# Linear attention inside a fused eleven-stage network: decays, heads and the norm of the memory set in another order

## What is computed

```python
def first_block(x, mem, mem_norm_g, norm_mix_g, ab_w_in, gla_w_alpha2, ...):
    mem_n = rms_norm(mem, mem_norm_g)
    ...
            proj = xn @ ab_w_in[j]
            y_a = gla_group(proj[..., :GLA_COLS], gla_w_alpha2[j], gla_b_alpha[j], gla_norm_g[j])
    ...
        h = h + mixed @ w_mix_out[layer]
        h = h + memory_cross_attention(rms_norm(h, norm_xattn_g[layer]), mem_n,
                                       xattn_wq[layer], xattn_wkv[layer], xattn_wo[layer])
```

## Time and profile before

| | |
|---|---|
| median of three runs | 3285.48 us (3285.32 to 3285.83) |
| the profiled execution's own time | 3284.78 us |
| its span in the trace | 3283.0 us |
| mean granted clock of TensorE | 0.98 of full |
| busy: PE / PEld / DVE / ACT / POOL | 95% / 76% / 47% / 36% / 4% |
| bytes moved | 270.60 MB, 82 GB/s over the span |

### The profile page before, as it was taken

How to read it: one execution, slowest core, us unless ns; L and a number is a source line. 1 busy time by engine, 2 the same in 40 slices (tenths; PEclk the granted TensorE clock), 3 DMA queues, 4 the chain that set the end, 5 groups by cost and what they waited for, 6 DMA issues and landing times.

```text
span 3283.0 us, 39941 instructions
## 1 busy us (share of the span) xinstructions
PE 3114.7 (95%) x17208; PEld 2490.4 (76%) x17208; DVE 1558.8 (47%) x1957; ACT 1175.8 (36%) x1564; POOL 126.5 (4%) x142
## 2 busy tenths in 40 slices
PE   8889988799999989899999998899999999999999
PEld 6787766577887766777887785588888887878887
DVE  4444446546544664546544654543335343363333
ACT  4343332434322464344322544532224322342221
POOL 1010000100000100100000200000001000000000
PEclk9899999899999999999999999999999999999999
DMA  4333001213332321313332231033323212133321
GB/s 150 119 131 104 15 21 40 77 52 90 103 90 85 94 64 52 103 42 97 92 97 78 91 90 52 26 94 98 93 87 116 81 64 93 65 103 90 103 90 64
DMA packets 355617, 270.60 MB, mean 82 GB/s; under 512 B 28672, under 2 KB 341504, under 8 KB 355184
## 3 DMA queue, kind: packets, MB, share of 16 engines
q1 hardware_dynamic: 351504, 252.83, 25.8%
q0 software_dynamic: 3936, 15.22, 1.3%
HBM read 261.73 MB, written 6.29 MB: 82 GB/s over the span
## 4 chain that ended last, share of the span: by engine, by line
PE 84%; DVE 8%; ACT 5%; issue 1%; POOL 0%; DMA 0%; DVEq 0%; SPq 0%; ACTq 0%; POOLq 0%
PE ps L189 83%; ACT arena L203 2%; DVE arena L220 2%; ACT whi L206 1%; DVE arena L212 1%; DVE wlo L212 1%; PE ps L192 1%; DVE hT L212 1%; DVE sml L229 1%; DVE xlo L220 1%; DVE arena L216 1%; ACT arena L206 0%; DVE split L212 0%; ACT L203 0%; POOL arena L212 0%
## 5 line engine op out<-in xcount | busy, mean ns | idle before, releaser
L189 PE MATMUL ps<-xhi,whi 128*128 128x512 f32 (+2 forms) x2192 | 874.1, 399 | 12.3 <-DVE wlo L212 4.2
L189 PE MATMUL ps<-xhi,wlo 128*128 128x512 f32 (+2 forms) x2192 | 857.1, 391 | 0.0
L189 PE MATMUL ps<-xlo,whi 128*128 128x512 f32 (+2 forms) x2192 | 856.7, 391 | 0.0
L189 PE MATMUL ps<-split,whi 128*128 128x512 f32 (+2 forms) x2640 | 830.9, 392 | 14.7 <-DVE split L212 10.4
L212 DVE TENSOR_TENSOR wlo<-wraw,whi 128x2048 fp32r<-128x2048 f32 (+4 forms) x258 | 550.7, 2137 | 475.6 <-ACT whi L206 475.4
L189 PEld LDWEIGHTS ps<-split,whi 128*128 128x128 f32 (+1 forms) x2640 | 491.5, 189 | 143.1 <-issue 26.6
L206 ACT ACTIVATE whi<-wraw 128x2048 fp32r<-128x2048 f32 (+4 forms) x258 | 456.2, 1771 | 352.8 <-PE ps L189 342.9
L189 PE MATMUL ps<-split,wlo 128*128 128x512 f32 (+2 forms) x1320 | 509.8, 386 | 0.0
L189 PEld LDWEIGHTS ps<-xhi,whi 128*128 128x128 f32 (+2 forms) x2192 | 410.9, 187 | 119.1 <-issue 10.4
L189 PEld LDWEIGHTS ps<-xhi,wlo 128*128 128x128 f32 (+2 forms) x2192 | 410.5, 187 | 91.9 <-issue 5.9
L189 PEld LDWEIGHTS ps<-xlo,whi 128*128 128x128 f32 (+2 forms) x2192 | 410.3, 187 | 90.6
(11 more groups left out here) (110 smaller groups left out, 2041.3 us busy)
## 6 DMA issues: line engine op xcount, KB each, us to landing
wraw<-in_ffn_w_up SPq DMA_DIRECT2D x128, 512.0 KB, 5.2
wraw<-in_ffn_w_down SPq DMA_DIRECT2D x32, 1024.0 KB, 5.0
wraw<-in_odd_w_in SPq DMA_DIRECT2D x24, 1024.0 KB, 5.2
wraw<-in_ffn_w_gate SPq DMA_DIRECT2D x44, 512.0 KB, 3.9
wraw<-in_xattn_wkv SPq DMA_DIRECT2D x16, 1024.0 KB, 5.6
wraw<-in_xattn_wq SPq DMA_DIRECT2D x8, 1024.0 KB, 5.1
wraw<-in_xattn_wo SPq DMA_DIRECT2D x8, 1024.0 KB, 5.2
wraw<-in_cd_w_in SPq DMA_DIRECT2D x8, 1024.0 KB, 5.6
```

The costliest lines, as they stand in the source:

```text
L189: return self.e.matmul(out, lhsT, rhs, start=start, stop=stop, skip_group_check=True)
```

## The change

In the stage gla, and nowhere else:

- The memory is normed before it is turned, while its tokens lie on the partitions: ACT takes the squares of two 128x1024 tiles with a sum along the row, and the root of the 128x2 sums; DVE scales both tiles by it. PE turns them when both are scaled. ACT rounds each turned tile with the gain as its scale, DVE makes its rest. The squares, products with ones, and eight products of the class Norm are gone.
- The values' product has 512 columns: two units of 512x512 rows and columns, 96 products, added up in four banks over both units. Both pairs' la products stand in it behind the first token tile of the first unit. The DVE and ACT work of both pairs' decays (decay) is issued at this place, between the roundings and rests of the units.
- The turnings ke and the updates U of both pairs stand between the gates' blocks; states(0) before the memory's first block on DVE, states(1) behind it.
- The heads' parts s, o and sum are set behind the memory's blocks 0 to 9 by a list (heads), so that part o of a head is two or more blocks behind its s, and its sum two behind its o; the other 22 blocks follow without a break. s no longer waits for the states.
- ke, SS, pts, EL, the squares, the roots and the outputs have two buffers each, in part on tiles that are free by then (la, keT, t1, ep).

The diff cut to its core:

```diff
-            la, t1, t2, ep, keT, U, SS, pts = (al(T), al(T), al(T), al(T), al(512), al(1024), al(1024), al(512))
-            os_, EL = la, sml[:, 16:24]
+            la, t1, ep, *ke = (al(T) for _ in range(5))
+            keT, U, SS, pts = al(512), al(1024), [al(1024), al(1024)], [al(512), al(512)]
+            sqs, rss, oss = [t1, ke[1]], [ep, ke[0]], [la, keT]
-            u_v = tm_units("v", Wi, 512, 512, 4)
+            u_v = [(("v", "unit", n), [(Wi[n * 512:n * 512 + 512, 512:1024], 0)], 512) for n in range(2)]
+                return ((("s", 0),), (("s", 1),), (("o", 0),), (("s", 2), ("o", 1)), (("sum", 0),), (("s", 3), ("o", 2)),
+                        (("sum", 1),), (("o", 3),), (("sum", 2),), (("sum", 3),))
...
+                    pe.wait_ge(S.V.of("mem", 1), ps.empty("turn", k))
...
+                bs = [ps.take("v", i, of=(0, 1, 2, 3)) for i in range(4)]
+                for n, (name, parts, bn) in enumerate(u_v):
+                    u = W.take(name, parts, bn)
+                    for i in range(4):
+                        c = slice(i * P, (i + 1) * P)
+                        pe.wait_ge(W.ready(name), ps.empty("v", i))
+                        for k in range(4):
...
+                        elif i == 0:
+                            decay(0)
+                            decay(1)
...
+                gates = fm_tensor(pe, S, u_g, X8, norm.made, of=(4, 5, 6, 7))
+                for p in range(2):
+                    next(gates)
+                    turn(p)
+                    next(gates)
+                    updates(p)
+                blocks = memory.tensor(pe)
+                for parts in heads():
+                    next(blocks)
+                    for what, hd in parts:
+                        part(what, hd)
+                run(blocks)
...
+                for i in range(2):
+                    dve.wait_ge(S.A.of("mem_root"))
+                    dve.ts(mt[:, i, :], mt[:, i, :], mem_rs[:, i:i + 1], None, ALU.mult).then_inc(*up(S.V, "mem", i))
+                W.rest(dve, u_qk[1][0])
+                W.rest(dve, u_a[0][0])
+                for k in range(8):
+                    dve.wait_ge(S.A.of("mem_hi", k))
+                    dve.stt(mem[k].lo, ps.ap("turn", k)[:, 0:256], par_col("mem_norm_g", None, k), mem[k].hi.bitcast(F32),
+                            ALU.mult, ALU.subtract).then_inc(*up(S.V, "mem_lo", k, frees=("turn", k)))
+                W.rest(dve, u_v[0][0])
...
+                decay(0)
+                W.rest(dve, u_v[1][0])
+                decay(1)
+                W.rest(dve, u_g[0][0])
+                states(0)
+                W.rest(dve, u_g[1][0])
+                blocks = memory.vector(dve)
+                next(blocks)
+                states(1)
+                for n, parts in enumerate(heads()):
+                    if n:
+                        next(blocks)
+                    for what, hd in parts:
+                        part(what, hd)
...
+                act.wait_ge(l_mem.of("x"))
+                for i in range(2):
+                    act.act(SS[i], mt[:, i, :], ACT.Square, acc=mem_rs[:, i:i + 1]).then_inc(*up(S.A))
+                act.wait_ge(S.A.own())
+                rstd_scalar(act, S, mem_rs, P, 2, 1024, 1e-6, mem_rs, None).then_inc(*up(S.A, "mem_root"))
...
+                for k in range(8):
+                    act.wait_ge(S.P.of("turn", k))
+                    act.copy(mem[k].hi, ps.ap("turn", k)[:, 0:256], scale=par_col("mem_norm_g", None, k)).then_inc(
+                        *up(S.A, "mem_hi", k))
+                W.round(act, u_v[0][0])
...
+                decay(0)
+                W.round(act, u_v[1][0])
+                decay(1)
+                for i in range(4):
+                    act.wait_ge(S.P.of("v", i))
+                    act.copy(vT[:, i * T:(i + 1) * T], ps.ap("v", i)).then_inc(*up(S.A, "v", i, frees=("v", i)))
...
+                for p in range(2):
+                    W.round(act, u_g[p][0])
+                    gate(2 * p)
+                    act.wait_ge(S.P.of("ke", p), S.P.of("U", 0, 1) if p else NEVER)
                     act.copy(keT, ps.ap("ke", p)).then_inc(*up(S.A, "keT", p, frees=("ke", p)))
+                    gate(2 * p + 1)
...
+                    elif what == "sum":
+                        act.wait_ge(S.P.of("sum", hd), S.V.of("mix", hd - 2) if hd > 1 else NEVER)
+                        rstd_scalar(act, S, ps.ap("sum", hd), P, T, P, 1e-6, rss[hd % 2], None).then_inc(
                             *up(S.A, "root", hd, frees=("sum", hd)))
                         act.wait_ge(S.V.of("mix", hd))
+                        act.copy(mixA[hd].hi, oss[hd % 2]).then_inc(*up(S.A, "mix_hi", hd))
```

More of the change, by code:

```diff
@@ L1208, in tensor @@
             def tensor(pe):
[L1209 to L1227, removed]
+                def run(stream):
+                    for _ in stream:
+                        pass
+                def decay(p):
+                    b = ps.take("la", p, of=(4, 5))
@@ L1237, in pair, with updates @@
                     i_.then_inc(*up(S.P, "ke", p))
[L1238 removed]
+                def updates(p):
                     for par_ in range(2):
[L1240 to L1241 removed]
+                        b = ps.take("U", p, par_, of=(2, 3))
+                        pe.wait_ge(S.A.of("keT", p), S.A.of("v", 3), ps.empty("U", p, par_))
                         r = par_ * 64
@@ L1248, in pair, with part @@
                         i_.then_inc(*up(S.P, "U", p, par_))
[L1249 to L1253, removed]
+                def part(what, hd):
+                    p, r0 = hd // 2, hd % 2 * 64
+                    q, k = qk[:, p * T:(p + 1) * T], qk[:, (2 + p) * T:(3 + p) * T]
+                    b = ps.take(what, hd, of=of)
+                    if what == "s":
+                        pe.wait_ge(S.V.of("ke", p), ps.empty("s", hd))
                         for i in range(4):
@@ L1270, in pair @@
                         pe.wait_ge(S.A.of("square", hd), ps.empty("sum", hd))
[L1271 to L1281, removed]
+                        i_ = pe.mm(b, ones, sqs[hd % 2])
@@ new lines, in part @@
+                    i_.then_inc(*up(S.P, what, hd))
+                run(fm_tensor(pe, S, u_qk, X8, norm.made, fresh=norm, sum_at=6))
+                run(fm_tensor(pe, S, u_a, X8, norm.made))
+                for k in range(8):
+                    b = ps.take("turn", k)
+                    pe.wait_ge(S.V.of("mem", 1), ps.empty("turn", k))
+                    for i in range(2):
+                        i_ = pe.tr(b[:, i * P:(i + 1) * P], mt[:, i, k * P:(k + 1) * P], ident)
+                    i_.then_inc(*up(S.P, "turn", k))
@@ new lines, in tensor @@
+                bs = [ps.take("v", i, of=(0, 1, 2, 3)) for i in range(4)]
[5 more added lines that the diff above has]
+                        for k in range(4):
+                            x = X8[4 * n + k]
+                            pe.wait_ge(norm.made(4 * n + k))
+                            pe.mm(bs[i], x.hi[:, c], u.hi[:, k, :], n == 0 and k == 0, False)
+                            pe.mm(bs[i], x.hi[:, c], u.lo[:, k, :], False, False)
+                            i_ = pe.mm(bs[i], x.lo[:, c], u.hi[:, k, :], False, n == 1 and k == 3)
+                        if n:
+                            i_.then_inc(*up(S.P, "v", i, unit=name if i == 3 else None))
+                        elif i == 0:
+                            decay(0)
+                            decay(1)
+                    if not n:
+                        i_.then_inc(*up(S.P, "v", "first", unit=name))
@@ L1327, in pair, with part @@
                                 U[:, c * P:(c + 1) * P], ALU.mult, ALU.add).then_inc(*up(S.V, "states", p))
[L1328 to L1332, removed]
-                               ALU.mult).then_inc(*up(S.V, "pts", hd, frees=("s", hd)))
[L1334 to L1339, removed]
+                def part(what, hd):
+                    if what == "s":
+                        dve.wait_ge(S.P.of("s", hd), S.P.of("o", hd - 2) if hd > 1 else NEVER)
+                        dve.tt(chunks(pts[hd % 2], 4), chunks(ps.ap("s", hd), 4), mi.unsqueeze(1).broadcast_to([P, 4, P]),
+                               ALU.mult).then_inc(*up(S.V, "pts", hd, frees=("s", hd)))
+                    elif what == "sum":
+                        o = oss[hd % 2]
+                        dve.wait_ge(S.A.of("root", hd), S.A.of("mix_hi", hd - 2) if hd > 1 else NEVER, S.V.own())
+                        dve.stt(o, ps.ap("o", hd), par_col("gla_norm_g", 0, hd), rss[hd % 2], ALU.mult, ALU.mult).then_inc(
@@ L1346, in both @@
[L1346 to L1350, removed]
+                        dve.tt(mixA[hd].lo, o, mixA[hd].hi.bitcast(F32), ALU.subtract).then_inc(*up(S.V, "mix_lo", hd))
+                decay(0)
[5 more added lines that the diff above has]
+                blocks = memory.vector(dve)
@@ L1351, in vector @@
+                next(blocks)
+                states(1)
```

(22 more changed lines are left out.)

120 lines of the change are left out of this document (41 added, 79 removed).

## The result

| | before | changed |
|---|---|---|
| median on one chip, us | 3285.65 (3285.32 to 3290.37) | 3247.37 (3243.68 to 3253.04) |
| profiled execution, us | 3284.78 | 3243.68 |
| start of the next stage, us of the span | 276.92 | 240.31 |
| PE products | 17208 | 17096 |

The change takes 38.3 us off, a ratio of 0.988 with a 95% interval of 0.9868 to 0.9892. The forecast was 3250.8 us with a range of 3243.8 to 3264: the time lies inside, 3.4 us under the forecast. A second and a third comparison of the same two kernels gave 3244.72 against 3286.80 and 3248.78 against 3286.03 us.

A forecast was written before the change was run, and what follows sets the result against it. PE, busy for 95% of the span, was taken as the bound. Gains of 23.8 + 4.4 + 0.7 + 8.2 = 37.1 us less 2.4 us gave 34.7 us net, so 3250.8 us, range 3243.8 to 3264.

The forecast's parts named there:

- The two long waits: PE's two waits for DVE's decays, 14.7 us together, go because each decay gets some 17 us of cover.
- The other waits: PE's waits for four sums (4.6 us), 2.3, 0.5, 0.9 and 0.78 us in the stage all go.
- The norm: Memory's norm: its products with ones, 4.4 us of PE, go; squares and scalings on ACT and DVE cost nothing.
- The values: Values' product: 96 products of 512 columns instead of 192 of 256 take 0.7 us less.
- The clock: Three stretches at half clock in the stage, 18.2 us of PE's work, go: 8.2 us won.
- The new waits: PE waits 2.1 us for block 12's weights behind head 3's end, and 0.3 us is added for the first values block.
- The sum: Gains of 37.1 us less 2.4 us of new waits: 34.7 us net.
- the first wait: Ahead of the first values product, for banks freed by rests on DVE: 0.3 us added, 0 to 1.
- The stage built up anew: Check adding up the stage's parts: it ends at 241.1 us against 276.9 before, 35.8 us less.
- a slow stretch behind the new wait: Rival: half clock behind the wait before block 12 costs 2.9 us more, 3253.7 us; chance 0.2.
- The heads' ends: Rival: all four hold ACT ahead of a rounding, with slow stretches, 17.9 us more, 3268.7, or half; chance 0.2.
- The dense blocks: Rival: weights bound the 16 memory and two output units; 2.4 us more per unit ends at 3294; chance 0.1.

The follow-up runs named there:

- The filled waits: Kernel before with seven and six useless products on PE in its two long waits: stage 256.7 us (-5.3), 3284.10 against 3288.45 us.
- late decays: Changed kernel with both decays' DVE and ACT work issued late: stage 245.9 us (+21.3), 3266.43 us against 3286.80 for the kernel before.
- the heads one apart: Changed kernel with s, o, sum of each head on three blocks in a row: stage 230.3 us (+5.7), 3251.77 us against 3288.45 for the kernel before.

## Why the prediction was right

*The two long waits.* Right, in size and mechanism: they are gone, each decay took 7.6 us on DVE and ACT (some 8 forecast), and with the cover taken away 14.2 us of waits come back, though not both at the turnings.

*The other waits.* All gone, as forecast. For the four sums the reason was wrong: "issued one block behind their o" is not what cost 1.16 us, the square's place behind a copy on ACT was.

*The norm.* The terms 4.4, 0.78 and 0.93 us, 6.1 together, measured 6.7. The squares that the trace had not shown took 1.04 us each (taken at 1.1), the scalings 0.75 each; nothing was paid for them.

*The values.* Mis-sized: 0.7 forecast, 1.3 measured.

*The clock.* 8.2 us forecast. The filled waits gave 47% of the slow work back; on 18.2 us that is 8.5, an estimate, since the wait of 2.25 us was not filled. The reason given was weaker than the size: "no wait over 2.5 us" has no row behind it, since one of the three stretches lay behind a wait of 2.25 us, and the wait of 2.34 us, longer than that one, is missing from its three longest. That no stretch came behind the new wait is in part luck: the same wait had one in two other kernels.

*The new waits.* 2.1 us forecast before block 12 and 2.06 measured, 0.3 ahead of the values and 0.68 measured. These rows of ACT in the changed kernel are the chain that was worked out for it, with head 3's root, its rounding and then the weights' (columns as in the earlier trace rows):

```profile
152.21 0.69 ACT L203 ACTIVATE arena<-ps,sml 128x512 f32<-128x512 f32 x1
152.93 0.63 ACT L203 ACTIVATE arena<-arena 128x512 f32<-128x512 f32 x1
155.11 0.63 ACT L206 ACTIVATE split<-arena 128x512 fp32r<-128x512 f32 x1 [1.54 <-DVE arena L212]
155.65 1.90 ACT L206 ACTIVATE whi<-wraw 128x2048 fp32r<-128x2048 f32 x1
```

*The sum.* 34.7 us forecast, 37.3 measured in the stage. The known differences are 0.6 for the norm, 0.6 for the values, 0.3 for the clock and -0.4 for the first wait, 1.1 in all. The other 1.5 us are about what the memory's 768 products took less, which the prediction put at nothing ("their returns to the other kind of product are as many as before"): counted from start to start and without waits they took 94.1 us in the changed kernel, and 97.7 in the kernel with filled waits, of which 4.2 were at half clock, so some 95.7 at full clock. Fewer blocks there stand beside another kind of product; that this is the cause is not shown. The stage built up anew, kept as a check, had said 35.8. The rest of the 38.3 us between the medians lies within the scatter of the later stages.

*The rivals.* No profile of the changed kernel had a slow stretch behind the new wait (none in three), but the kernels with late decays and with the heads one apart had one behind the same wait: two of the six profiles with that wait. 0.2 was a fair chance for it. The heads' ends held PE once, not four times. The dense blocks were not bound by weights: 2.85 us a block at 230 GB/s.

## What to carry to other kernels

Where PE bounds a kernel, look for long chains of small operations on other engines and issue them while PE has products that do not need them; the wait is only part of the price, since here the lower clock around two of them, 14.7 us together, added 5.3 us. Find the place of a short wait on the in-order engine that releases it: a square behind a copy cost 1.16 us four times, and moving the product further off was not what cured it. Where later stages scatter by several us, compare starts of stages in traces, and not times, for an edit of 2 or 3 us.

## What was not expected of the hardware

The granted clock fell to half in stretches of 3.4 us behind waits of only 1.36, 2.05 and 2.06 us, and did not fall behind the wait of 2.06 us in four other profiles, nor behind the one of some 2.34 us at 33 us in any of thirteen. What PE does next may count as well: behind the waits of 1.36 and 2.25 us it first made a head's output, 22 small products in 2.8 and 3.9 us, and behind the 2.34 us products of 512 columns. No run separates the wait's length from this. The Trainium skill ("TensorE: Matmul & The Clock Gate", section "What's actually happening") says that the window over which PE's activity is watched is free-running and does not reset with a kernel's start; that the same wait is followed by a slow stretch in one profile and not in another agrees with it. Seven products of ones with an fp32 tile, 6.17 us in all, kept the clock at 1.00 around the wait of 7.7 us, which had a slow stretch without them.
